# Six of a feed-forward block's last eight output tiles computed by Strassen's scheme, and two small pieces of work moved ahead of them

## The chip, the cores and the metric

The kernel runs on one core of a Trainium2 chip. The metric is the device time of one execution in microseconds (us), of which there are three for the kernel before. The program runs five engines side by side, which meet only at semaphores: TensorE (PE in the rows; PEld is its weight load), VectorE (DVE), ScalarE (ACT), GpSimd (POOL) and SyncE (SP), whose queue issues nearly all DMAs.

## The reference

Two transformer blocks run in sequence on 512 tokens of width 1024. The part in question is the feed-forward part of the first, and one norm of the second:

```
def _sq_relu_mlp(h, w1, w2):                       # w1: 1024 x 4096, w2: 4096 x 1024
    return jnp.square(jax.nn.relu(h @ w1)) @ w2
...
    y_x = _sq_relu_mlp(_modulate(x, g_pre_mlp[l], sh2, sc2), w_mlp_in[l], w_mlp_out[l])
    x = x + gt2 * _rmsnorm(y_x, g_post_mlp[l])
...
def mem_group(q_raw, mem_h, w_mem_kv, q_norm, k_norm):     # 256 memory rows, 4 heads of 128
    ...
    k = rmsnorm(kv[:, :, 0], k_norm)
...
    lb_all = jnp.cumsum(jax.nn.softmax(hg_lb_logits.astype(jnp.float32), axis=0), axis=0)
```

The first product gives 4096 inner features, the second sums over them to 1024 outputs. The memory keys are normed over 128 features per head. The "lower bounds" are a softmax over two rows of 512 numbers.

## The kernel before

**Numbers.** Activations lie transposed: 128 features on the partitions, tokens along the row. A product keeps float32 accuracy with three TensorE matmuls in the type fp32r: each operand is split into a high part (ACT copies it to fp32r) and a low part (the rest, subtracted by POOL or DVE), and `products` (L879, L880, L881) issues high x high, low x high and high x low into one PSUM bank. A plain output tile of 128 features is summed over its input tiles k in matmuls of 512 columns, one for each token.

**Strassen pairs.** Most tiles of the MLP are computed in pairs of output tiles by a scheme of seven products in place of eight: two output tiles by two halves of the tokens, over even and odd input tiles. A pair issues 7 products of 4 input pairs of 3 matmuls of 256 columns, that is 84. For each pair the other engines prepare seven weight pieces: `weight_sums` (DVE, L3087 to L3097) forms four sums of weight tiles; `piece_high` (ACT, L1824) copies the seven pieces q = 0 to 6 to fp32r; `piece_rest` (POOL, L3814) subtracts for q = 0, 1, 3, 5, 6 and `piece_low` (DVE, L2750) for q = 2, 4. Afterwards `first_product` (ACT), `product_sums` and `first_sum` (DVE, L3110 to L3122) join the seven products to two output tiles. ACT's copy of piece q for the next pair overwrites the buffer of piece q of the running pair, so it waits for that product:

```
            else:
                act.wait_ge(s.prod, 7 * (n - 1) + q + 1)
```

**The loop.** `FIRST_MLP` lists the pairs n = 0 to G-1. It goes in quarters of the 4096 inner features: "inner" pairs (two tiles of 128 features each, k from 2c to 2c+1, called c) and then "outer" pairs, which add a quarter's eight input tiles into all eight output tiles of `y`. Before, outer pairs 0 to 11 belong to quarters 0 to 2, four each; `OUTER[d]` is the place of outer pair d in the list, `INNER[p]` of inner pair p. An outer pair that comes first in its quarter (`first_out`: d = 0, 4, 8) issues three quarters of each product, and then the last quarters. ACT, DVE and POOL each run one loop over n with their work written out in order by hand; within iteration n they prepare pair n+1's pieces.

For an inner result of quarters 0 to 2, ACT squares (`even_squared`, `odd_squared`) and splits it, DVE adds four sums of 256 columns for the scheme's inputs (`form_sums`, L3197 to L3203), ACT copies them high (`sums_of_form_high`) and POOL subtracts twice (`form_sums_rest`, ySL). For quarter 3 (c = 12 to 15) it is split whole into `bH` and `bL` and no sums are formed.

**The last quarter's output.** Its eight tiles m = 0 to 7 are plain: m = 0 and 1 together, then 2 to 5, each 8 k of 3 matmuls of 512 columns; then m = 6 and 7 for the first 256 tokens and for the others, so that the norm of the first half can start. `ahead` splits chunks of 8 weight tiles (ACT L1815, POOL L3809). DVE adds each bank to `y` (L3288, L3306), ACT squares it, POOL sums the squares (`add_squares`, L3819, and `late_squares`). `half_statistic` (L1355, L1356) puts the sum over features on PE in the fifth step of tile 6's second half; then ACT takes the root, and `second_norm` (DVE L3320, L3323, L3328, ACT L1826) makes the next block's input from `y` and `xT`.

**What lies between those tiles.** After tiles 1 to 4, PE issues `statistic_of_halves("mk0".."mk3", 256)` (L951, L952): ones times the high and low parts of a head's squared keys. ACT squares and splits, DVE takes the rest (`low_sums`), ACT the root, DVE scales the key (L3294). The lower bounds take nine instructions on [128, 4] or [128, 8] (DVE L3270 to L3283, ACT L2279, L2280) ahead of tile 0's addition.

**SP's queue.** `weights_load(i)` loads 512 KB into one of four buffers `raw` once it is free. The residual `xT` (2 MB) is reloaded from DRAM ahead of load `last_inner`, after outer pair 11. It shares its memory with `yS`, the forms of an outer quarter.

Of the kernel before, what the change touches and what calls it, by code (L numbers as in the profile page):

```python
# [53 lines left out]
OUT_ORDER = [24 + i for i in (0, 1, 2, 3, 4, 5, 7, 6)]  # L54


def plan_weights():
# [73 lines left out]
    for c in range(0, len(plan), CB):  # L131
# [15 lines left out]
             + [("outer", 4 * quarter + j) for j in range(4 if quarter < 3 else 0)]]  # L147
# [210 lines left out]
def after_run(n):  # L358

    return len(SPLIT) if run_of(n) else number("w_mlp_out", OUT_ORDER[0], 0)  # L360
# [168 lines left out]
def _banks():  # L529
# [54 lines left out]
def build(nc, xt, xn, ctxt, memt, pos, wall, vec, cst, invc, hmask, rpbw, poolw, out):  # L584
# [275 lines left out]
    def tensor_program():  # L860
# [85 lines left out]
        def statistic_of_halves(name, n=512):  # L946
            o = claim(7)
# [381 lines left out]
        def XB(k):  # L1329
            return bH[:, k % 8, :], bL[:, k % 8, :], s.lo, LO.b + (k if k % 2 else k + 2)  # L1330

        outs = [claim(BANK["w_mlp_out", m]) for m in range(2)]
        for i, k in enumerate(OUT_ORDER):
            x_h, x_l, sem, value = XB(k)
            pe.wait_ge(sem, value)
            for m in range(2):
                w_h, w_l, raise_ = weights("w_mlp_out", k, m)
                mm = products(outs[m], w_h, w_l, x_h, x_l, i == 0, i == 7)
                if raise_:
                    mm.then_inc(s.product, 1)  # L1340
# [453 lines left out]
    def scalar_program():  # L1794
# [375 lines left out]
        def odd_high(c):  # L2170
# [5 lines left out]
            if c < 12:  # L2176
                copy(yH[:, c % 4, 256:768], squares_of(c)[1], s.hi)
            else:
                copy(bH[:, 2 * (c - 12) + 1, :], squares_of(c)[1], s.hi)

        def even_high(c):
            if c:
                act.wait_ge(s.relu_sq, 2 * c)
            if c < 12:
                copy(yH[:, c % 4, 0:256], squares_of(c)[0][:, 0:256], s.hi)
            else:
                copy(bH[:, 2 * (c - 12), :], squares_of(c)[0], s.hi)
# [2162 lines left out]
```

## Time and profile before

| | us |
|---|---|
| three runs | 1290.13, 1290.35, 1290.64 |
| median | 1290.35 |
| the profiled execution's own time | 1291.04 |
| its span | 1289.7 |
| PE busy in the span | 1278.8 |
| DVE, ACT, POOL busy | 964.3, 782.5, 807.2 |

The profile is of one execution. Its span runs from the first to the last instruction; its own time holds 1.34 us more. Times in its rows are from the span's start. A matmul's duration counts its way through the array, so the cost of one in a row of them is the distance from its start to the next start. "[0.81 <-PE bank L881]" behind a row says how long the engine was idle before it, and what ended that.

### The profile page before, as it was taken

The page shows a single profiled execution, that of the slowest core. Times are in us where ns is not written, and L with a number is a line of the kernel's source. Part 1 is how long each engine was busy: PE and PEld are TensorE (multiplying, and loading weights), DVE is VectorE, ACT ScalarE, POOL GpSimd, SP SyncE. Part 2 cuts the span into 40 slices and gives each one's busy share as a digit, 9 for nine tenths or more (in the row PEclk, how much of TensorE's full clock was granted, in tenths as well). Part 3 has the DMA queues.
Part 4 walks back from the last instruction along what each step waited for, and adds up shares of the span by engine and source line. Part 5 has one row for each costly group of instructions (what it writes and reads, how often), then busy time and mean ns, then how long its engine had stood idle before and what let it go on. Part 6 is the DMA issues. An engine that isn't in the chain of part 4 may idle for free.

```text
span 1289.7 us, 22877 instructions
## 1 busy us (share of the span) xinstructions
PE 1278.8 (99%) x8718; PEld 1136.6 (88%) x8718; DVE 964.3 (75%) x1692; ACT 782.5 (61%) x1488; POOL 807.2 (63%) x585
## 2 busy tenths in 40 slices
PE   9999999999999999999999999999999999999998
PEld 6788778879999999988788788777789999999998
DVE  5796695878778989834468575747589887987888
ACT  4532585479677585865655557645577655765664
POOL 3643333579778687656467373644378876877785
DMA  9685235353333323533332112120223333333333
GB/s 378 240 323 203 88 127 209 126 176 107 115 107 99 110 102 100 180 99 101 128 108 81 45 63 67 65 66 33 66 82 115 99 99 105 107 101 116 99 106 108
DMA packets 42125, 156.35 MB, mean 121 GB/s; under 512 B 4384, under 2 KB 5152, under 8 KB 40992
## 3 DMA queue, kind: packets, MB, share of 16 engines
q1 hardware_dynamic: 41136, 151.60, 34.2%
q0 software_dynamic: 448, 2.62, 0.5%
q8 instruction: 69, 1.13, 0.3%
q10 hardware_dynamic: 432, 0.67, 0.1%
q14 instruction: 40, 0.33, 0.1%
HBM read 149.90 MB, written 4.19 MB: 119 GB/s over the span
## 4 chain that ended last, share of the span: by engine, by line
PE 82%; DVE 10%; ACT 4%; POOL 2%; issue 2%; DMA 1%; DVEq 0%; SPq 0%; POOLq 0%; ACTq 0%
PE bank L879 23%; PE bank L881 22%; PE bank L880 22%; PE bank L1437 2%; PE bank L928 1%; PE bank L929 1%; PE bank L930 1%; PE bank L982 1%; DVE small L2940 1%; POOL wL L3814 1%; PE bank L942 1%; PE bank L975 1%; DVE P L2948 1%; PE bank L967 1%; PE bank L1674 1%
## 5 line engine op out<-in xcount | busy, mean ns | idle before, releaser
L3809 POOL TENSOR_TENSOR wL<-raw,wH 128x1024 fp32r<-128x1024 f32 (+1 forms) x91 | 223.3, 2459 | 239.9 <-ACT wH L1815 236.8
L879 PE MATMUL bank<-hH,wH 128*128 128x512 f32 (+1 forms) x544 | 211.0, 388 | 1.6 <-POOL wL L3809 0.6
L881 PE MATMUL bank<-hH,wL 128*128 128x512 f32 (+1 forms) x544 | 200.6, 369 | 0.0
L880 PE MATMUL bank<-hL,wH 128*128 128x512 f32 (+1 forms) x544 | 200.3, 368 | 0.0
L3814 POOL TENSOR_TENSOR wL<-raw,wH 128x512 fp32r<-128x512 f32 (+1 forms) x120 | 154.3, 1286 | 31.2 <-ACT wH L1824 30.5
L879 PE MATMUL bank<-gH,wH 128*128 128x256 f32 x512 | 145.4, 284 | 0.3 <-POOL gL L3814 0.3
L881 PE MATMUL bank<-gH,wL 128*128 128x256 f32 x512 | 144.9, 283 | 0.0
L880 PE MATMUL bank<-gL,wH 128*128 128x256 f32 x512 | 144.9, 283 | 0.0
L1815 ACT ACTIVATE wH<-raw 128x1024 fp32r<-128x1024 f32 (+1 forms) x91 | 95.1, 1047 | 53.7 <-PE bank L881 27.5
L879 PEld LDWEIGHTS bank<-hH,wH 128*128 128x128 f32 x544 | 102.9, 189 | 24.9 <-issue 6.5
L881 PEld LDWEIGHTS bank<-hH,wL 128*128 128x128 f32 x544 | 102.6, 189 | 18.0
L880 PEld LDWEIGHTS bank<-hL,wH 128*128 128x128 f32 x544 | 103.0, 189 | 15.3 <-issue 1.9
L3814 POOL TENSOR_TENSOR wL<-t,wH 128x512 fp32r<-128x512 f32 (+1 forms) x66 | 83.4, 1264 | 26.3 <-ACT wH L1824 25.9
L879 PEld LDWEIGHTS bank<-gH,wH 128*128 128x128 f32 x512 | 98.3, 192 | 0.7 <-POOL gL L3814 0.5
L2750 DVE TENSOR_TENSOR wL<-bank,wH 128x512 fp32r<-128x512 f32 (+1 forms) x118 | 79.7, 675 | 25.6 <-ACT wH L1824 25.6
L880 PEld LDWEIGHTS bank<-gL,wH 128*128 128x128 f32 x512 | 98.3, 192 | 0.2 <-issue 0.2
L881 PEld LDWEIGHTS bank<-gH,wL 128*128 128x128 f32 x512 | 98.3, 192 | 0.0
L3814 POOL TENSOR_TENSOR pL<-raw,pH 128x512 fp32r<-128x512 f32 (+1 forms) x60 | 77.4, 1289 | 27.8 <-ACT pH L1824 27.3
L1824 ACT ACTIVATE wH<-bank 128x512 fp32r<-128x512 f32 (+1 forms) x118 | 69.2, 586 | 42.1 <-DVE bank L3093 27.2
L1824 ACT ACTIVATE wH<-raw 128x512 fp32r<-128x512 f32 (+1 forms) x120 | 74.5, 621 | 33.2 <-PE bank L881 32.1
L3814 POOL TENSOR_TENSOR wL<-tmp,wH 128x512 fp32r<-128x512 f32 x52 | 67.8, 1304 | 25.4 <-ACT wH L1824 24.4
L879 PE MATMUL bank<-yH,wH 128*128 128x256 f32 x288 | 81.5, 283 | 0.0
(538 smaller groups left out, 4072.4 us busy)
## 6 DMA issues: line engine op xcount, KB each, us to landing
raw<-in_wall SPq DMA_DIRECT2D x211, 512.0 KB, 3.3
rows<-in_wall SPq DMA_DIRECT2D x24, 1024.0 KB, 11.3
bra<-in_rpbw SPq DMA_DIRECT2D x8, 360.0 KB, 4.5
xq<-in_xt SPq DMA_DIRECT2D x2, 1024.0 KB, 6.6
xT<-in_xn SPq DMA_DIRECT2D x1, 2048.0 KB, 7.9
out_x<-xT SPq DMA_DIRECT2D x1, 2048.0 KB, 8.8
xT<-out_x SPq DMA_DIRECT2D x1, 2048.0 KB, 9.2
out_x<-xT SPq DMA_DIRECT2D x6, 256.0 KB, 2.4
```

Source lines behind the costliest of these rows:

```text
L879: matmul(o, a_h, b_h, start=first, stop=False)
L880: matmul(o, a_h, b_l, start=False, stop=False)
L881: return matmul(o, a_l, b_h, start=False, stop=last)
L928: matmul(o, x_h, w_h, start=n == 0, stop=False)
L929: matmul(o, x_h, w_l, start=False, stop=False)
L930: mm = matmul(o, x_l, w_h, start=False, stop=n == len(ks) - 1)
L1437: mm = matmul(o[:, 64 * c:64 * c + 64], e_[:, 128 * c:128 * c + 128], view(e_[:, :], 128 * c + m, [[2 * m, 64 // m], [1, m]]), start=True, ...
L1815: activation(wH[i % NHL][:, 0:n], raw[r % NRAW][:, 0:n], ACT.Copy).then_inc(s.w_hi, 1)
L1824: activation(dst, src, ACT.Copy).then_inc(sem, 1)
L2750: tt(low, src, high.bitcast(F32), ALU.subtract).then_inc(sem, 1)
L3809: tt(wL[i % NHL][:, 0:n], raw[load(c) % NRAW][:, 0:n], wH[i % NHL][:, 0:n].bitcast(F32), ALU.subtract).then_inc(s.w_lo, 1)
L3814: tt(low, src, high.bitcast(F32), ALU.subtract).then_inc(sem, 1)
```

## The change

- **Outer pairs 12, 13 and 14** (output tiles 0 to 5 of the last quarter) join the loop; pair 12 is a `first_out` one, and the last of the loop is outer pair 14 and no longer inner pair 13. Tiles 6 and 7 stay plain and in halves. Inner results c = 12 to 15 get the sums of forms as all others. Since m = 6, 7 want the plain late tokens of the even tiles, these go to `xlast`, and ACT (`late_high`) and POOL split them (`xlH`, `xlL`, 128 x 1024) in iteration `OUTER[13]`.
- **Squares of y** follow as `result_square` (ACT) and `result_sum` (POOL) in the order `Y_ORDER`, with buffers `ysum` and `ysq` of their own.
- **The memory keys' norm** moves into quarter 0. ACT squares and splits all four heads at once at the end of iteration `OUTER[0]` (`memory_squares`, two instructions of 128 x 1024). POOL subtracts at the end of iteration `OUTER[1]`. PE issues the statistic in two parts of 512 columns, `mk0` after product q = 0 of `OUTER[2]` and `mk1` after product q = 0 of `OUTER[3]`. ACT takes the roots after `first_product` there and DVE scales (`memory_key`) before `product_sums`.
- **The lower bounds** become a generator of five steps, run after `OUTER[1]`, `[4]`, `[6]`, `[8]`, `[11]` on DVE, with ACT's two exponentials at the end of `OUTER[3]`.
- **SP:** the reload of `xT` goes as two DMAs of 1 MB, ahead of load `first_f + 2`, after `s.prod >= 7 * G`. The two loads of `hmask` wait for `xlL` in place of `mk3`. POOL's DMA of the positions waits for `mk1`.

```diff
@@ plan_weights
-        if quarter < 3:
-            for j in range(4):
-                for i, odd in ((0, 0), (1, 0), (1, 1), (0, 1)):
-                    tile("w_mlp_out", 2 * j + i, range(8 * quarter + odd, 8 * quarter + 8, 2))
-        else:
-            group([("w_mlp_out", m) for m in range(2)], OUT_ORDER)
-            for m in range(2, 8):
-                tile("w_mlp_out", m, OUT_ORDER)
+        for j in range(4 if quarter < 3 else 3):
+            for i, odd in ((0, 0), (1, 0), (1, 1), (0, 1)):
+                tile("w_mlp_out", 2 * j + i, range(8 * quarter + odd, 8 * quarter + 8, 2))
+    for m in (6, 7):
+        tile("w_mlp_out", m, OUT_ORDER)
@@ tensor_program
+        KEY_PLACE = {(OUTER[2], 0): 0, (OUTER[3], 0): 1}
+
+        def memory_statistic(i):
+            statistic_of_halves(f"mk{i}", 512, BANK["mk", i])
+            freed[BANK["mk", i]] = s.mk_n, 2 * i + 2
...
                     product_of(n, q, range(4), True, True).then_inc(s.prod, 1)
+                if (n, q) in KEY_PLACE:
+                    memory_statistic(KEY_PLACE[n, q])
...
-        for m in range(6):
-            b = BANK["w_mlp_out", m]
-            if m >= 2:
-                tile("w_mlp_out", m, OUT_ORDER, [(claim(b), XB)])
-            freed[b] = s.y_full, m + 1
-            if 0 < m < 5:
-                statistic_of_halves(f"mk{m - 1}", 256)
@@ scalar_program
+        def late_high():
+
+            act.wait_ge(s.relu_sq, 2 * 15)
+            act.wait_ge(s.prod, 7 * (INNER[13] + 1))
+            copy(xlH[:, :, :], xlast[:, :, :], s.full)
+
+        def memory_squares():
+            act.wait_ge(s.k_mem, 4)
+            activation(ksq[:, :], kvM[:, 0:2, :].rearrange("p a t -> p (a t)"), ACT.Square).then_inc(s.head_sq, 4)
+            act.wait_ge(s.head_sq, 4)
+            activation(ksqH[:, :], ksq[:, :], ACT.Copy).then_inc(s.sums_hi, 2)
+
+        def memory_root(i):
+            root_of(f"mk{i}", 128, bank[BANK["mk", i]], bank[BANK["mk", i]])
+
+        def result_square(i):
+
+            act.wait_ge(s.y, Y.half + 24 + i + 1)
+            if i > 2:
+                act.wait_ge(s.add_g, ADD_G.f + i - 2)
+            square((ysq[i % 2] if i else ysum)[:, :], y[:, Y_ORDER[i], :], s.sq)
...
             first_product(n)
+            if outer_of(n) in (2, 3):
+                memory_root(outer_of(n) - 2)
             piece_high(n + 1, 2)
...
+            if outer_of(n) == 13:
+                late_high()
             piece_high(n + 1, 3)
...
             piece_high(n + 1, 6)
+            if outer_of(n) == 13:
+                result_square(0)
+                result_square(1)
...
             if n + 2 < G:
                 even_columns(n + 2)
+            if outer_of(n) == 0:
+                memory_squares()
@@ vector_program
+        def memory_key(i):
+            dve.wait_ge(s.root, rooted(f"mk{i}"))
+            dve.wait_ge(s.ones, 5)
+            stt(out=kvM[:, i, :], in0=kvM[:, i, :], scalar=vc("mem_k"), in1=bank[BANK["mk", i]],
+                op0=ALU.mult, op1=ALU.mult).then_inc(s.mk_n, 2)
...
                 piece_low(n + 1, 2)
+            if outer_of(n) in (2, 3):
+                memory_key(outer_of(n) - 2)
             product_sums(n)
@@ gpsimd_program
+        def result_sum(i):
+            pool.wait_ge(s.sq, SQ.f + i + 1)
+            if i > 1:
+                pool.wait_ge(s.add_g, ADD_G.f + i - 1)
+            tt(ysum[:, :], ysum[:, :], ysq[i % 2][:, :], ALU.add).then_inc(s.add_g, 1)
...
             piece_rest(n + 1, 3)
+            if outer_of(n) == 13:
+                pool.wait_ge(s.full, FULL.b + 33)
+                rest(xlL[:, :, :], xlast[:, :, :], xlH[:, :, :], s.rest_g)
...
             piece_rest(n + 1, 5)
             piece_rest(n + 1, 6)
...
+            if outer_of(n) == 1:
+                pool.wait_ge(s.sums_hi, halved("mk1") + 1)
+                tt(ksqL[:, :], ksq[:, :], ksqH[:, :].bitcast(F32), ALU.subtract).then_inc(s.sums_lo, 2)
@@ sync_program
-            if i == last_inner:
-                sp.wait_ge(s.prod, outer_done(2))
+            if i == first_f + 2:
+                sp.wait_ge(s.prod, 7 * G)
                 sp.wait_ge(s.x_moved, 32)
-                nc.sync.dma_start(xT[:, :, :], out).then_inc(s.x_moved, 16)
+                nc.sync.dma_start(xT[:, 0:4, :], out[:, 0:4, :]).then_inc(s.x_moved, 16)
+                nc.sync.dma_start(xT[:, 4:8, :], out[:, 4:8, :]).then_inc(s.x_rest_in, 16)
```

## Rows read from the trace of the kernel before

**Rows 1.** The page: head, busy time, and the chain that ended last.

```profile
span 1289.7 us, 22877 instructions
PE 1278.8 (99%) x8718; PEld 1136.6 (88%) x8718; DVE 964.3 (75%) x1692; ACT 782.5 (61%) x1488; POOL 807.2 (63%) x585
PE 82%; DVE 10%; ACT 4%; POOL 2%; issue 2%; DMA 1%; DVEq 0%; SPq 0%; POOLq 0%; ACTq 0%
```

**Rows 2.** Busy time by stretches: an inner pair of quarter 2; the six tiles.

```profile
core 0: us, PE busy (x) PEld busy (x) DVE busy (x) ACT busy (x) POOL busy (x), PEclk, DMA share, GB/s
558.59:592.29 33.70, 33.70 (x154) 27.98 (x153) 10.15 (x24) 17.91 (x34) 20.33 (x11) 1.00 0.31 104
447.50:457.60 10.10, 10.10 (x86) 10.10 (x86) 8.63 (x18) 8.90 (x18) 7.30 (x7) 1.00 0.34 105
```

**Rows 3.** PE's timeline around tiles 0 to 5 (start, duration, engine).

```profile
558.47 0.28 PE L881 MATMUL bank<-hH,wL 128*128 128x256 f32 x1
558.59 0.40 PE L879 MATMUL bank<-bH,wH 128*128 128x512 f32 x1
...
569.49 0.28 PE L951 MATMUL bank<-sumH,ones 128*128 128x256 f32 x1
569.61 0.28 PE L952 MATMUL bank<-sumL,ones 128*128 128x256 f32 x1
569.73 0.40 PE L879 MATMUL bank<-bH,wH 128*128 128x512 f32 x1
...
592.29 0.28 PE L879 MATMUL bank<-bH,wH 128*128 128x256 f32 x1
592.41 0.28 PE L880 MATMUL bank<-bL,wH 128*128 128x256 f32 x1
```

**Rows 4.** PE's timeline where outer pairs 1, 9 and 2 start.

```profile
325.88 0.28 PE L881 MATMUL bank<-yH,wL 128*128 128x256 f32 x1
326.10 0.39 PE L879 MATMUL bank<-yH,pH 128*128 128x256 f32 x1
326.32 0.28 PE L880 MATMUL bank<-yA,pH 128*128 128x256 f32 x1
...
487.53 0.28 PE L881 MATMUL bank<-yH,wL 128*128 128x256 f32 x1
487.93 0.39 PE L879 MATMUL bank<-yH,pH 128*128 128x256 f32 x1
...
336.27 0.28 PE L879 MATMUL bank<-yH,pH 128*128 128x256 f32 x1
337.71 0.28 PE L879 MATMUL bank<-yH,wH 128*128 128x256 f32 x1
```

**Rows 5.** ACT's timeline in iteration `OUTER[1]`, and a chunk's copy.

```profile
330.31 0.61 ACT L1824 ACTIVATE pH<-raw 128x512 fp32r<-128x512 f32 x1
336.47 0.63 ACT L1824 ACTIVATE wH<-tmp 128x512 fp32r<-128x512 f32 x1 [0.81 <-PE bank L881]
...
553.31 1.05 ACT L1815 ACTIVATE wH<-raw 128x1024 fp32r<-128x1024 f32 x1
```

**Rows 6.** POOL's timeline in iteration `OUTER[1]`, and a chunk's rest.

```profile
331.01 1.31 POOL L3814 TENSOR_TENSOR pL<-raw,pH 128x512 fp32r<-128x512 f32 x1
332.26 1.33 POOL L3814 TENSOR_TENSOR wL<-raw,wH 128x512 fp32r<-128x512 f32 x1
337.18 1.30 POOL L3814 TENSOR_TENSOR wL<-tmp,wH 128x512 fp32r<-128x512 f32 x1
...
554.43 2.40 POOL L3809 TENSOR_TENSOR wL<-raw,wH 128x1024 fp32r<-128x1024 f32 x1 [3.73 <-ACT wH L1815]
```

**Rows 7.** The whole span's waits of PE's weight load: us in total, times, longest.

```profile
PEld bank L1046 <- DVE xsq L2806: 2.0, 2, 1.5
```

**Rows 8.** The norm behind tiles 6 and 7: PE, DVE and POOL.

```profile
599.85 0.59 PE L1355 MATMUL bank<-acc,ones 128*128 128x256 f32 x2
...
602.47 0.43 DVE L3323 TENSOR_TENSOR bank<-xT,bank 128x256 f32<-128x256 f32 x1
...
593.99 1.29 POOL L3819 TENSOR_TENSOR acc<-acc,tmp 128x512 f32<-128x512 f32 x1 [1.61 <-ACT tmp L1839]
```

**Rows 9.** The page's DMA issues: KB each, median us from issue to landing.

```profile
rows<-in_wall SPq DMA_DIRECT2D x24, 1024.0 KB, 11.3
xq<-in_xt SPq DMA_DIRECT2D x2, 1024.0 KB, 6.6
xT<-out_x SPq DMA_DIRECT2D x1, 2048.0 KB, 9.2
```

More of the change, by code:

```diff
@@ L50 @@
 GROUPS = ((0, 8), (8, 16), (16, 22))
-OUT_ORDER = [24 + i for i in (0, 1, 2, 3, 4, 5, 7, 6)]
+OUT_ORDER = range(24, 32)
+Y_ORDER = (1, 0, 3, 2, 5, 4)
 def plan_weights():
@@ L146 @@
              for pair in [("inner", p) for p in range(max(0, 4 * quarter - 2), 4 * quarter + 2)]
-             + [("outer", 4 * quarter + j) for j in range(4 if quarter < 3 else 0)]]
+             + [("outer", 4 * quarter + j) for j in range(4 if quarter < 3 else 3)]]
 INNER = {i: at for at, (kind, i) in enumerate(FIRST_MLP) if kind == "inner"}
@@ L358, in after_run @@
 def after_run(n):
[L360 removed]
+    return len(SPLIT) if run_of(n) else number("w_mlp_out", OUT_ORDER[0], 6)
 def reach(name, k, m, chunks=NHL):
@@ L441 @@
 MULT = before(hc=8, h2=8, b=3)
-FULL = before(first=16, hm=8, h2=4, b=24, fs=22)
+FULL = before(first=16, hm=8, h2=4, b=33, fs=22)
 REST = before(first=8, hm=4, h2=8, fs=22)
-REST_G = before(first=8, hm=4, s2=4, b=24, form=4, fb=22)
+REST_G = before(first=8, hm=4, s2=4, b=33, form=4, fb=22)
 X2_S = before(x2=8, up=22)
@@ L458, in normed @@
     return NORMS.index((which, j - j % 2))
-ROOTS = ("x ctx mem mix pre_mlp mk0 mk1 mk2 mk3 post_a post_b h3 mq hg0 hg1 hg2 hg3 lq lk q k "
+ROOTS = ("x ctx mem mix pre_mlp mk0 mk1 post_a post_b h3 mq hg0 hg1 hg2 hg3 lq lk q k "
          "om ol ffn").split()
@@ L469, in rooted @@
     return 2 * ROOTS.index(name) + 2
-HALVED = "mk0 mk1 mk2 mk3 lq".split()
+HALVED = "mk0 mk1 lq".split()
 def halved(name):
@@ L552, in _banks @@
         of.update((("sum", p, j), of["sum", p - (2 - j // 2), (1, 3, 0, 2)[j]]) for j in range(4))
-    held = [of["sum", G - 2, 1], of["sum", G - 2, 3], of["sum", G - 1, 2]]
-    of.update((("w_mlp_out", m), b) for m, b in enumerate(held + held + [2, 3]))
+    of.update({("w_mlp_out", 6): 2, ("w_mlp_out", 7): 3})
+    of.update({("mk", i): of["sum", OUTER[2 + i] - 1, 1] for i in range(2)})
     of.update({("vt", 0): 4, ("vt", 1): 6})
@@ L678, in build @@
     xl = at("xl", R + 92 * K, [128, 256])
+    xlast = at("xl", 88 * K, [128, 4, 256])
+    xlH = at("xlH", R + 56 * K, [128, 4, 256], F32R)
+    xlL = at("xlL", R + 60 * K, [128, 4, 256], F32R)
+    ysum = at("ysum", R + 72 * K, [128, 512])
+    ysq = [at("ysq", R + (74 + 2 * i) * K, [128, 512]) for i in range(2)]
     sS = [at("sS", R + (24 + 4 * i) * K, [128, 1024]) for i in range(2)]
@@ L1327, in tensor_program, with XB @@
             first_freed(n)
[L1329 to L1340, printed above, removed]
-        for m in range(6):
-            b = BANK["w_mlp_out", m]
-            if m >= 2:
-                tile("w_mlp_out", m, OUT_ORDER, [(claim(b), XB)])
-            freed[b] = s.y_full, m + 1
-            if 0 < m < 5:
-                statistic_of_halves(f"mk{m - 1}", 256)
+        def XB(k, i):
+            c = 12 + (k - 24) // 2
+            if k % 2:
+                return yH[:, c % 4, 256 + 256 * i:512 + 256 * i], yB[c % 4][:, i, :], s.lo, LO.b + 2 * c + 1
+            if i:
+                return xlH[:, c % 4, :], xlL[:, c % 4, :], s.rest_g, REST_G.b + 33
+            return yH[:, c % 4, 0:256], yA[c % 4][:, :], s.lo, LO.b + 2 * c + 2
         freed[2] = freed[3] = s.piece_v, 2 * G
@@ L2175, in odd_high @@
             forms_free(c)
[L2176 to L2179, printed above, removed]
+            copy(yH[:, c % 4, 256:768], squares_of(c)[1], s.hi)
         def even_high(c):
@@ L2183, in even_high @@
                 act.wait_ge(s.relu_sq, 2 * c)
[L2184 to L2187, printed above, removed]
+            copy(yH[:, c % 4, 0:256], squares_of(c)[0][:, 0:256], s.hi)
         def sums_of_form_high(c, side):
@@ L3184, in form_sums @@
             x_, y_ = squares_of(c)
-            late = xl[:, :] if c else tm[1][:, 256:512]
+            late = tm[1][:, 256:512] if c == 0 else xl[:, :] if c < 12 else xlast[:, c - 12, :]
             s1, s4, s3, s2 = (yS[c % 4][:, 256 * n:256 * n + 256] for n in range(4))
@@ L3947, in gpsimd_program @@
             if n + 1 == G:
-                ahead("w_mlp_out", 24, 0, 2)
+                result_sum(1)
+                ahead("w_mlp_out", OUT_ORDER[0], 6, 2)
+                result_sum(2)
+                result_sum(3)
                 continue
@@ L3958, in gpsimd_program @@
             piece_rest(n + 1, 6)
-        for m in range(8):
-            if m not in (1, 7):
-                ahead("w_mlp_out", OUT_ORDER[4 if m == 0 else 0], m)
-            if 0 < m < 6:
-                if m > 1:
-                    pool.wait_ge(s.add_g, ADD_G.f + m - 1)
-                add_squares(acc[0][:, :], m, s.sq, SQ.f)
+            if outer_of(n) == 1:
+                pool.wait_ge(s.sums_hi, halved("mk1") + 1)
+                tt(ksqL[:, :], ksq[:, :], ksqH[:, :].bitcast(F32), ALU.subtract).then_inc(s.sums_lo, 2)
+        result_sum(4)
+        result_sum(5)
         def late_squares(i):
```

191 lines of the change are left out of this document (79 added, 112 removed).

## The prediction, on record before the changed kernel was run

> **What bounds the kernel.** I read the page's head first: TensorE is busy for 1278.8 of 1289.7 us, and the chain that ended last is PE for 82% [rows 1]. Then the stretches: in an inner pair of quarter 2 and in the six tiles PE is busy for the whole stretch at the granted clock 1.00, that is 2.4 GHz, while POOL has 2.8 to 13 us left [rows 2]. So a us of matmuls taken away is a us of span, and a wait that PE did not have is lost whole: no later wait of PE is long enough to take it up, the longest of its weight load being 1.5 us in the whole span, and none of any size lies in the first MLP [rows 7, 4]. The question is then how many us of matmuls go, and whether PE meets a new wait.
>
> **The matmuls removed and added.** The six tiles are 6 x 8 x 3 = 144 matmuls of 512 columns and the four statistics 8 of 256. They stand from 558.59 to 592.29: 33.70 us. The first 48 take 569.49 - 558.59 = 10.90, so 0.227 us each; one of 256 columns takes 0.120 (569.49 to 569.61) [rows 3]. 144 x 0.227 + 8 x 0.12 = 33.65, which closes. In their place come 3 pairs x 84 x 0.120 = 30.24, and 4 statistic matmuls of 512 columns in quarter 0, 4 x 0.227 = 0.91. That is -33.70 + 30.24 + 0.91 = -2.55 us. So Strassen's eighth is only 2.5 us here: a matmul half as wide costs more than half.
>
> The rule for back-to-back matmuls in the Trainium skill ("TensorE: Matmul & The Clock Gate", section on the back-to-back issue gap) is columns / 2.4 + 2.5 ns, 216 ns for 512 columns and 109 for 256. The trace disagrees by 11 ns at both widths. An estimate by that page would be 144 x 0.216 + 8 x 0.109 = 31.98 before and 252 x 0.109 + 4 x 0.216 = 28.33 after, -3.6 in place of -2.55, and the total below would be 1291.2. I take the trace.
>
> **A small wait behind a first outer pair.** Where a pair follows a `first_out` one, POOL has two ySL subtractions ahead of the new pair's piece 0, and PE starts late: outer pair 1 by 326.32 - 325.88 - 0.24 = 0.20 us, outer pair 9 by 0.40 + 0.22 - 0.24 = 0.38 with the same slow second start [rows 4]. Outer pair 13 is now such a pair. Bounds 0.20 and 0.38; quarter 3 is like quarter 2, so near the upper, +0.3.
>
> **The statistic in `OUTER[2]`: a new wait.** PE issues mk0 behind product 0 of outer pair 2, and it needs ksqL, which POOL makes at the end of iteration `OUTER[1]`, behind piece 6 of pair 2. ACT's copy of piece 6 waits for the last product of outer pair 1. The trace shows this wait end at 336.47, just behind the end of that pair; POOL's subtraction starts at 337.18 and takes its turn of 1.26 [rows 5, 6]. PE, though, starts pair 2 at 336.27 and is done issuing product 0 at 337.71 [rows 4]. The work that PE needs can't even begin by then.
>
> When does it end? I move the engines' rows by what is inserted.
> ACT: `memory_squares` starts where the copy of piece 0 now stands, 330.31. Each of its two instructions is 128 x 1024 from SBUF, for which the nearest row is 1.05 [rows 5]; with the wait of the second for the first, the copy of piece 0 starts at 332.4 and ends at 333.0.
> POOL: piece 0 at 333.1 (now 331.01), then pieces 1, 3, 5, 6 back to back at turns of 1.25 (331.01 to 332.26) [rows 6]: piece 6 at 338.1, ksqL at 339.35. ACT has made up its delay by piece 6, for which it waits anyway. ksqL is a subtraction of 128 x 1024 as at 554.43, 2.40 [rows 6]: it ends at 341.75.
> PE goes on at 341.75 and pays 0.1 for a weight load that couldn't run ahead, as at 326.10 to 326.32 [rows 4]. PE's loss is 341.85 - 337.7 = 4.15 us.
> Bounds: if `memory_squares` cost POOL nothing, ksqL would run from 338.45 to 340.85, 3.2 us of wait. If POOL's and ACT's new instructions took half as long again in company, it is 4.15 + 1.2 + 1.0 = 6.4. I take the worked value. Behind PE only TensorE's own products wait; the other engines use the time to get ahead, so nothing else grows. Nothing brings it back either.
>
> **What I cost at nothing, and its cover.**
> mk1 in `OUTER[3]`: its low part comes with mk0's. It claims the bank of pair 2's sum, which ACT copies to `y` some 0.2 us before PE comes: between 0 and 0.3.
> ACT's two roots and DVE's two scalings: each 0.6 to 0.9 us, in outer pairs of quarter 0 where ACT waits for PE 0.8 us at a time [rows 5]; DVE's `product_sums` moves by 0.8, but its result is wanted by ACT only 1.4 later. Without that cover a bank comes late by 0.8.
> The lower bounds: nine instructions of 0.15 to 0.2 us, one to three per outer pair. Tile 0's addition is gone, behind which they were hidden before, so nothing is saved.
> Forms of quarter 3: DVE +4 sums of 256 columns, POOL +2 subtractions, ACT +2 copies per inner pair. That is what quarter 2 does already, where DVE is busy for 8.63, ACT for 8.90 and POOL for 7.30 of 10.10 and PE does not wait [rows 2].
> Iteration `OUTER[13]`: ACT +1.05 (`late_high`) and two squares, POOL +2.40 (xlL) between pieces 3 and 5. Piece 6 is then ready some 3 us into pair 14 and wanted after 8.6. The chunk of tile 6 is ready on POOL 1.7 us before PE reaches it.
> The norm's chain: PE comes to `half_statistic(0)` at 599.85, 7.56 behind the start of tile 6 at 592.29 [rows 8, 3]. Now four more sums of 1.29 [rows 8] stand on POOL behind the chunk of tile 7, and end 5.8 behind that start; the last two squares need 0.7 more, so 6.8 with ACT: 0.8 to spare. If the spare is gone, each us over it is a us of span.
> SP: the reload of xT starts when tile 6 does and is wanted 602.47 - 592.29 = 10.2 later [rows 8, 3]. 1 MB landed in 6.6 (xq), 2 MB in 9.2 (xT), 1 MB in a crowd in 11.3 (rows) [rows 9]: hidden, or 1.1 late at worst. The weight loads `first_f + 2`, `+ 3` and the hmask loads now queue behind it, and land by some 14 us after tile 6's start; ACT takes them at 15 and 17.
>
> **The sum.** -2.55 + 0.30 + 4.15 = +1.9 us. The profiled execution (span 1289.7, own time 1291.04) would become 1291.6 and 1292.9. Its own time is 0.69 above the median of the runs; the difference carries over: 1290.35 + 1.9 = **1292.25 us**.
>
> About 0.2%, 2.6 us, is what a measurement of this kernel can tell from no change. The forecast lies inside.
>
> **The rivals.**
> A, on the other side (slower): the clock. PE has never stood for 4 us in this trace; through all waits up to 1.5 the granted clock stayed 1.00 [rows 7, 2]. If this wait lets it fall to 1.2 GHz, the products behind it take double: 12 x 0.12 = 1.44 more for one product at that clock, 2.9 for two. Total +3.3 to +4.8: 1293.7 to 1295.1. It decides from 0.7 us on, six matmuls at half clock. For: the length of the wait. Against: before and behind it PE is busy without a break.
> The Trainium skill ("TensorE: Matmul & The Clock Gate", Part 1 on the clock gate) states that the clock halves after an idle stretch and is given back after sustained work. No run here shows it yet; by that rule rival A is what happens, if 4 us is idle enough.
> B (slower): one of the covers fails: DVE in quarter 3, which starts behind three bound steps, the norm's chain, or xT. Each is worth 1 to 2 us: about 1293.8. For: the spare of the norm's chain and of xT is worked out, not seen. Against: every one has a row of a like stretch that keeps time.
> C: the wait isn't there, because ksqL is done in time. Then -2.25: 1288.1, still within 0.2%. For: nothing but that POOL's spans are rough. Against: ACT's wait at 336.47 [rows 5] holds it whatever POOL's speed.
> D (faster by over 0.2%): no wait, and the norm's chain gains as well, since tile 6's neighbours leave ACT and POOL more room: 1287 or less.
>
> **How the numbers follow.** Forecast 0.56, A 0.19, B 0.12, C 0.08, D 0.05. A tenth of the forecast's own cases (a wait above 4.8) lies over +2.6. Slower by over 0.2%: 0.19 + 0.12 + 0.05 = 0.36. Faster: 0.05. Within: 0.59. The range leaves out C and D (0.13) below and the far end of A above: from 1290.3 (the wait at its lower bound of 3.2, the step behind pair 12 at 0.2, less 0.9 for what else is off) to 1295.2 (A with two products). The forecast's own range is 1291.3 to 1294.5, from the two bounds of the wait.
>
> **What would show it.** In the new profile: three more pairs of 10.1 us on PE; tile 6 starting 30.5 us behind the end of inner pair 13; in quarter 0 PE idle once for about 4 us, behind product 0 of the outer pair 2 near 338 us, ended by POOL's subtraction of 128 x 1024; two matmuls of 512 columns behind it; the second statistic without a wait; the granted clock in the 10 us behind it (1.00 for the forecast, less for A); the distance from tile 6's start to L1355 still 7.6 us. The prediction is wrong if the wait isn't there or is half as long, or if pairs of quarter 3 take more than 10.1 us.

## The result, and the profile after

The changed kernel takes 1297.78 us (median of six runs, 1296.92 to 1298.53), the kernel before 1290.30 (six runs, 1290.12 to 1291.00): ratio 1.0055, 95% interval 1.0044 to 1.0066. That is 7.5 us slower. I had forecast 1292.25, with a range to 1295.2.

The page's head, the counterpart of [rows 1]:

```profile
span 1296.0 us, 23202 instructions
PE 1281.1 (99%) x8822; PEld 1143.2 (88%) x8822; DVE 989.5 (76%) x1735; ACT 791.7 (61%) x1512; POOL 825.8 (64%) x604
PE 74%; DVE 14%; ACT 5%; issue 3%; POOL 3%; DMA 1%; DVEq 0%; SPq 0%; ACTq 0%; POOLq 0%
```

PE's share of the chain that ended last fell from 82% to 74%, and DVE's rose from 10% to 14%. That is a hint that more than one long wait happened: the chain leaves PE more often.

To find where, I follow PE's starts, as in [rows 3, 4], at the forecast wait (start, duration, engine):

```profile
336.78 0.28 PE L889 MATMUL bank<-yH,pL 128*128 128x256 f32 x1
341.02 0.77 PE L959 MATMUL bank<-ksqH,ones 128*128 128x512 f32 x1 [3.96 <-POOL ksqL L3974]
341.58 0.63 PE L960 MATMUL bank<-ksqL,ones 128*128 128x512 f32 x1
342.01 0.42 PE L887 MATMUL bank<-yH,wH 128*128 128x256 f32 x1
...
346.91 0.28 PE L889 MATMUL bank<-yH,wL 128*128 128x256 f32 x1
...
598.63 0.28 PE L887 MATMUL bank<-yH,wH 128*128 128x256 f32 x1
...
606.19 0.67 PE L1360 MATMUL bank<-ysum,ones 128*128 128x256 f32 x2
```

The wait is 341.02 - 336.78 - 0.12 = 4.12 us, ended by `ksqL`, the POOL subtraction named in the prediction. But behind it the distance from start to start is 0.21 in place of 0.12. Windows over the same stretch show why:

```profile
336.90:341.00 4.10, 0.16 (x2) 0.01 (x1) 4.07 (x5) 1.43 (x3) 4.10 (x4) 0.89 0.39 128
341.00:347.00 6.00, 5.98 (x26) 5.82 (x27) 3.07 (x5) 1.23 (x2) 2.39 (x2) 0.51 0.28 90
347.00:357.00 10.00, 10.00 (x84) 9.91 (x83) 6.56 (x12) 7.05 (x13) 5.19 (x4) 1.00 0.17 52
```

The column behind POOL's is the granted clock: 0.51 from 341 to 347, which is the 1.2 GHz level, and 1.00 again from 347. The two matmuls of 512 columns take 342.01 - 341.02 = 0.99 in place of 2 x 0.227, and the 23 behind them 346.91 - 342.01 = 4.90 in place of 23 x 0.12 = 2.76. Together that is 0.54 + 2.14 = 2.68 us. Of these, 0.11 is not the clock's: behind a wait at the full clock the same two matmuls take 0.57 and not 0.454 (342.39 - 341.82 in the second experiment), which is the 0.1 that the prediction counted for a weight load that can't run ahead. The clock's own part is 2.57. The Trainium skill ("TensorE: Matmul & The Clock Gate", Part 1) says that the clock halves after an idle stretch and returns after sustained work; the trace agrees, with 0.51 behind 4.12 us of standing still and 1.00 behind the 5.9 us of work that followed.

POOL's timeline, the counterpart of [rows 6], has the order that I worked out, all of it some 0.8 us earlier, as PE's pairs are here in this execution:

```profile
332.29 1.29 POOL L3814 TENSOR_TENSOR pL<-raw,pH 128x512 fp32r<-128x512 f32 x1 [2.00 <-ACT pH L1830]
...
337.31 1.27 POOL L3814 TENSOR_TENSOR wL<-tmp,wH 128x512 fp32r<-128x512 f32 x1
338.53 2.34 POOL L3974 TENSOR_TENSOR ksqL<-ksq,ksqH 128x1024 fp32r<-128x1024 f32 x1
```

DVE's timeline has rows that I had no term for. The first two are steps of the lower bounds behind `OUTER[1]`, the next three those behind `OUTER[4]` and `OUTER[6]`; the row at 446.41 is three steps of the positions' angles, which stood behind `OUTER[7]` before as well, and the last is where `product_sums` of inner pair 7 starts:

```profile
337.41 1.19 DVE L3239 TENSOR_TENSOR lb<-vecs,lb 128x4 f32<-128x4 f32 x1
338.52 2.37 DVE L3240 TENSOR_TENSOR lb<-vecs,lb 128x4 f32<-128x4 f32 x1
...
417.94 0.92 DVE L3243 TENSOR_TENSOR lb<-lb 128x4 f32<-128x4 f32 x1
418.90 0.18 DVE L3245 RECIPROCAL lb<-lb 128x4 f32<-128x4 f32 x1
...
438.09 0.76 DVE L3248 TENSOR_TENSOR lb<-lb 128x4 f32<-128x4 f32 x1
...
446.41 4.69 DVE L3151 SCALAR_TENSOR_TENSOR tmp<-tmp 128x512 f32<-128x512 f32 x3
...
465.78 0.41 DVE L3113 TENSOR_TENSOR acc<-bank,rs 128x256 f32<-128x256 f32 x1
```

A subtraction of 4 elements per partition takes 2.37 us, and it ends at 340.89, when POOL's `ksqL` ends (338.53 + 2.34 = 340.87); the one ahead of it ends at 338.60, and POOL's piece at 338.58. The same instructions in the kernel before took 0.155 and 0.161, at 562 us, where POOL had nothing to do. The kernel before, POOL's timeline there:

```profile
564.63 4.75 POOL L3809 TENSOR_TENSOR wL<-raw,wH 128x1024 fp32r<-128x1024 f32 x2 [5.11 <-ACT wH L1815]
```

and operations on `lb`, by line:

```profile
L3272 DVE TENSOR_TENSOR lb<-vecs,lb x1: 161/161/161, 562.3 to 562.3; 128x4 f32<-128x4 f32 x1
L3273 DVE TENSOR_TENSOR lb<-vecs,lb x1: 155/155/155, 562.4 to 562.4; 128x4 f32<-128x4 f32 x1
L3275 DVE TENSOR_TENSOR lb<-lb x1: 163/163/163, 562.9 to 562.9; 128x4 f32<-128x4 f32 x1
...
L3281 DVE TENSOR_SCALAR lb<-lb x1: 169/169/169, 563.5 to 563.5; 128x4 f32<-128x4 f32 x1
```

(The three numbers are the shortest, median and longest duration in ns, then follow the first and last start.) Finally PE's new short waits in quarters 2 and 3, the rows that have a releaser:

```profile
464.99 0.38 PE L887 MATMUL bank<-hH,pH 128*128 128x256 f32 x1 [0.49 <-DVE yB L2753]
...
495.81 0.39 PE L887 MATMUL bank<-yH,wH 128*128 128x256 f32 x1 [0.28 <-POOL ySL L3814]
497.05 0.39 PE L887 MATMUL bank<-yH,pH 128*128 128x256 f32 x1 [0.27 <-POOL pL L3814]
...
578.37 0.39 PE L887 MATMUL bank<-yH,pH 128*128 128x256 f32 x1 [0.26 <-POOL pL L3814]
```

Each costs what its start lies too late, and 0.10 more, since the next start is 0.22 behind it, as in [rows 4]. In quarter 2 the seven of them (464.99: 0.74; 475.16 and 485.32: 0.08 each; 493.18: 0.34; 494.55: 0.31; 495.81: 0.54; 497.05: 0.53) make 2.62, of which 0.38 was there before [rows 4, outer pair 9]: 2.24. In quarter 3 two (577.13: 0.16; 578.37: 0.52) make 0.68.

So from the last matmul of outer pair 0 (325.07) to the first of tile 6 (598.63) 273.56 us pass, where it was 592.29 - 325.88 = 266.41 [rows 3, 4]. The 7.15 us are -2.55 + 4.12 + 2.68 + 2.24 + 0.68 = 7.17. Behind tile 6 nothing moved: from there to the end of the span are 697.37 us, before 697.41. The difference of the spans is 6.3 and not 7.15 because outer pair 0 ended 0.8 earlier in the execution profiled after. That execution's own time, 1297.33, is 0.45 below its median, and the one before was 0.69 above: 6.3 + 0.45 + 0.69 is the 7.4 to 7.5 between the medians.

### The profile page after: what moved, and what is told of

Read it like the earlier page. It is cut to its first block, busy times and chain, and to the rows that moved or that the text cites. A ratio compares the mean times of both kernels' runs of the same rounds, so it can differ in the third digit from the quotient of the medians.

```text
span 1296.0 us, 23202 instructions
## 1 busy us (share of the span) xinstructions
PE 1281.1 (99%) x8822; PEld 1143.2 (88%) x8822; DVE 989.5 (76%) x1735; ACT 791.7 (61%) x1512; POOL 825.8 (64%) x604
## 3 DMA queue, kind: packets, MB, share of 16 engines
q0 software_dynamic: 448, 2.62, 0.5%
## 4 chain that ended last, share of the span: by engine, by line
PE 74%; DVE 14%; ACT 5%; issue 3%; POOL 3%; DMA 1%; DVEq 0%; SPq 0%; ACTq 0%; POOLq 0%
PE bank L887 20%; PE bank L889 19%; PE bank L888 19%; PE bank L1443 2%; PE bank L936 1%; PE bank L938 1%; PE bank L937 1%; PE bank L990 1%; DVE bank L3118 1%; DVE small L2943 1%; PE bank L950 1%; DVE bank L3096 1%; PE bank L983 1%; POOL wL L3814 1%; PE bank L975 1%
## 5 line engine op out<-in xcount | busy, mean ns | idle before, releaser
L3809 POOL TENSOR_TENSOR wL<-raw,wH 128x1024 fp32r<-128x1024 f32 (+1 forms) x85 | 208.7, 2460 | 223.0 <-ACT wH L1821 219.9
L3814 POOL TENSOR_TENSOR wL<-raw,wH 128x512 fp32r<-128x512 f32 (+1 forms) x126 | 162.3, 1289 | 32.2 <-ACT wH L1830 31.7
L1821 ACT ACTIVATE wH<-raw 128x1024 fp32r<-128x1024 f32 (+1 forms) x85 | 89.0, 1048 | 53.7 <-PE bank L889 27.5
L887 PE MATMUL bank<-yH,wH 128*128 128x256 f32 x384 | 110.2, 287 | 0.3 <-POOL ySL L3814 0.3
L889 PE MATMUL bank<-yH,wL 128*128 128x256 f32 x384 | 109.6, 285 | 0.0
L2753 DVE TENSOR_TENSOR wL<-bank,wH 128x512 fp32r<-128x512 f32 (+1 forms) x124 | 83.7, 675 | 33.2 <-ACT wH L1830 33.2
L1830 ACT ACTIVATE wH<-bank 128x512 fp32r<-128x512 f32 (+1 forms) x124 | 72.7, 587 | 47.8 <-DVE bank L3096 34.2
L3814 POOL TENSOR_TENSOR pL<-raw,pH 128x512 fp32r<-128x512 f32 (+1 forms) x63 | 81.2, 1289 | 28.8 <-ACT pH L1830 28.2
L1830 ACT ACTIVATE wH<-raw 128x512 fp32r<-128x512 f32 (+1 forms) x126 | 78.3, 621 | 32.5 <-PE bank L889 31.3
```

The costliest lines, as they stand in the source:

```text
L887: matmul(o, a_h, b_h, start=first, stop=False)
L889: return matmul(o, a_l, b_h, start=False, stop=last)
L1821: activation(wH[i % NHL][:, 0:n], raw[r % NRAW][:, 0:n], ACT.Copy).then_inc(s.w_hi, 1)
L1830: activation(dst, src, ACT.Copy).then_inc(sem, 1)
L2753: tt(low, src, high.bitcast(F32), ALU.subtract).then_inc(sem, 1)
L3809: tt(wL[i % NHL][:, 0:n], raw[load(c) % NRAW][:, 0:n], wH[i % NHL][:, 0:n].bitcast(F32), ALU.subtract).then_inc(s.w_lo, 1)
```

## The experiments

Theories ahead of them: the long wait costs its 4.1 and a fallen clock 2.7 (W with the clock); the lower bounds, stretched by POOL, make DVE late in quarter 2 (L); against L, that quarter 2's waits are a late effect of the stop at 341, which shifted the engines against each other (K). In the expectations below, C is the rival that the clock falls for another reason than the wait.

### The keys' low part ahead of pair 2's pieces

```diff
@@ gpsimd_program, iteration OUTER[1]
+            if outer_of(n) == 1:
+                pool.wait_ge(s.sums_hi, halved("mk1") + 1)
+                tt(ksqL[:, :], ksq[:, :], ksqH[:, :].bitcast(F32), ALU.subtract).then_inc(s.sums_lo, 2)
             piece_rest(n + 1, 0)
             piece_rest(n + 1, 1)
...
             piece_rest(n + 1, 6)
-            if outer_of(n) == 1:
-                pool.wait_ge(s.sums_hi, halved("mk1") + 1)
-                tt(ksqL[:, :], ksq[:, :], ksqH[:, :].bitcast(F32), ALU.subtract).then_inc(s.sums_lo, 2)
```

> The changed kernel with one instruction moved on GpSimd: the low part of the squared keys is taken ahead of the first piece of outer pair 2 and not behind its last. Theory W (PE's one wait in outer pair 2, and the fall of the clock behind it, cost 4.1 + 2.7 us; the short waits of quarters 2 and 3, some 2.8 us, have another cause): no idle time of PE above 0.5 us in outer pair 2, granted clock 1.00 there, 1297.8 - 6.9 = 1290.9 us. Rival K (the later short waits are knock-on effects of that wait): they go too, 1289 us or less, or 1288.5. Rival C (the clock falls for another reason than the wait): 1293.6.

Measured: 1291.81 us (1291.03 to 1292.13) beside 1290.40 for the kernel before, ratio 1.0009 (1.0000 to 1.0017). From the changed kernel's time that is -6.0. POOL's timeline:

```profile
332.44 2.41 POOL L3962 TENSOR_TENSOR ksqL<-ksq,ksqH 128x1024 fp32r<-128x1024 f32 x1 [1.57 <-ACT ksqH L2208]
334.81 1.30 POOL L3814 TENSOR_TENSOR pL<-raw,pH 128x512 fp32r<-128x512 f32 x1
```

and PE's:

```profile
337.84 0.50 PE L959 MATMUL bank<-ksqH,ones 128*128 128x512 f32 x1
...
459.55 0.38 PE L887 MATMUL bank<-hH,pH 128*128 128x256 f32 x1 [0.42 <-DVE yB L2753]
```

The wait and the half clock (4.12 + 2.68 = 6.80) are gone, and the granted clock is 1.00 over the whole execution; a late piece 0 takes 0.27 of it back, and the two statistics 0.20 and 0.41, by the distances of PE's starts. 6.80 - 0.88 = 5.9. K falls: without any stop in quarter 0, the wait on `yB` in inner pair 8 is still there (0.42), and `product_sums` of inner pair 7 starts 11.45 us into its pair, as after the change (11.51: 465.78 less the pair's start of 454.27), where the kernel before had 9.33.

### Sixteen matmuls in the wait

```diff
@@ tensor_program, memory_statistic
+            if i == 0:
+                o = claim(BANK["mk", 0])
+                pe.wait_ge(s.sums_hi, halved("mk1") + 1)
+                for _ in range(16):
+                    matmul(o, ones_r[:, :], HALVES["mk0"][1], start=True, stop=True)
```

> The changed kernel with its wait left in place, but PE kept busy through it: ahead of the wait for the low part it issues 16 matmuls of 512 columns (3.6 us) into the bank that the statistic overwrites. The output is unchanged. Theory W: PE goes on at the same time as in the changed kernel, some 4 us late, but at the full clock; only the clock's part comes back, -2.7: 1295.1 us. Rival C (the clock falls for another reason, or the products behind the wait are slow for want of operands): about 1297.8.

Measured: 1294.61 us (1294.52 to 1295.58), ratio 1.0034 (1.0021 to 1.0047); -3.2 from the changed kernel. PE's timeline, and the window behind it:

```profile
337.59 0.28 PE L889 MATMUL bank<-yH,pL 128*128 128x256 f32 x1
338.06 3.92 PE L1326 MATMUL bank<-ksqH,ones 128*128 128x512 f32 x16 [0.19 <-ACT y L1835]
341.82 0.50 PE L959 MATMUL bank<-ksqH,ones 128*128 128x512 f32 x1
342.16 0.40 PE L960 MATMUL bank<-ksqL,ones 128*128 128x512 f32 x1
342.39 0.28 PE L887 MATMUL bank<-yH,wH 128*128 128x256 f32 x1
```

```profile
342.00:348.00 6.00, 6.00 (x49) 5.91 (x50) 3.42 (x6) 3.75 (x7) 2.32 (x2) 1.00 0.26 90
```

The statistic comes 341.82 - 337.59 = 4.23 us behind product 0, to be read beside 4.24 after the change: the wait is whole, but PE has work in it, and the clock stays at 1.00. From product 0's last matmul to tile 6 the trace is 2.66 us shorter than the changed kernel's (596.78 - 337.59 = 259.19 beside 598.63 - 336.78 = 261.85): the 2.57 worked out from the rows, and nearly 0.1 of shorter waits in quarter 2. So 2.6 us are the clock's, and they can be had back without touching the wait. The medians differ by 0.5 more than the rows explain; the five runs lie 1.1 us apart.

### The lower bounds in quarter 0

```diff
@@ vector_program
-            if outer_of(n) in (1, 4, 6, 8, 11):
-                next(bound)
+            for _ in range({1: 1, 3: 4}.get(outer_of(n), 0)):
+                next(bound)
@@ scalar_program
-            if outer_of(n) == 3:
+            if outer_of(n) == 2:
```

> The changed kernel, wait included, with the five steps of the lower bounds put into quarter 0 alone (one behind outer pair 1, four behind outer pair 3; ACT's exponentials behind outer pair 2). Theory L (small VectorE instructions with both operands in SBUF wait for GpSimd's running instruction, 0.5 to 1.2 us each, and in quarters 1 and 2 VectorE has no time left): product_sums at the start of quarter 2 comes 9.3 us and not 11.4 into a pair, the waits of PE between 460 and 498 us shrink from 2.3 to 0.4 us: 1297.8 - 1.9 = 1295.9 us. Rival K (those waits follow from the long wait in outer pair 2): 1297.8.

Measured: 1295.11 us (1293.98 to 1295.67), ratio 1.0035 (1.0022 to 1.0049); -2.7 from the changed kernel. `product_sums` of inner pair 7 starts 9.32 into its pair again (463.95 - 454.63), and of quarter 2's waits one is left, that which the kernel before had. DVE's timeline, and PE's:

```profile
463.95 0.41 DVE L3113 TENSOR_TENSOR acc<-bank,rs 128x256 f32<-128x256 f32 x1
```

```profile
494.83 0.28 PE L889 MATMUL bank<-yH,wL 128*128 128x256 f32 x1
495.25 0.39 PE L887 MATMUL bank<-yH,pH 128*128 128x256 f32 x1
```

From product 0's last matmul to tile 6 it is 2.21 us less than after the change (259.64), as the 2.24 of quarter 2 would have it. The instructions were not made shorter but put where DVE has time: there the multiplication (L3248) took 1.20 us, and nobody waited for it.

### Both

The first experiment's edit and the third's together.

> Both edits together: the keys' low part early on GpSimd, and the lower bounds in quarter 0. Theories W and L: only the waits behind the first outer pairs are left, so -2.55 for the columns and +0.7 for quarter 3 against the kernel of before: about 1288.8 us (1288.3 to 1289.5). If a cost of the change has been missed: 1290 or more.

Measured: 1288.99 us (1288.57 to 1289.54) beside 1290.40, ratio 0.9990 (0.9981 to 0.9998). This is faster than both kernels, than the one before by an interval that just leaves out 1. Its rest is explained by its rows: -2.55 for the columns; a late piece 0 in outer pair 2 (336.26) 0.26, the two statistics 0.20 and 0.04; the step in quarter 3 0.72. That sums to -1.33, measured -1.4.

The 0.04 at the second statistic shows something that the first experiment hid, where it was 0.41. There the second subtraction of the lower bounds behind `OUTER[1]` took 1.33 us beside POOL's piece, and here, in the same place, 0.15: it starts at 339.80, and POOL's piece at 339.82. In the first experiment they start at 339.82 and 339.84. What decides between 0.15 and 1.33 is less than these rows resolve. With the 1.33, DVE is 1.2 us later at the end of outer pair 2, and ACT's copy that frees the bank of the second statistic is late: this bound step costs PE 0.37 where PE does not stand in `OUTER[2]`.

### The keys' low part in the middle of the pieces

```diff
@@ gpsimd_program, iteration OUTER[1]
                 form_sums_rest(c, 1)
+            if outer_of(n) == 1:
+                pool.wait_ge(s.sums_hi, halved("mk1") + 1)
+                tt(ksqL[:, :], ksq[:, :], ksqH[:, :].bitcast(F32), ALU.subtract).then_inc(s.sums_lo, 2)
             piece_rest(n + 1, 5)
             piece_rest(n + 1, 6)
-            if outer_of(n) == 1:
-                pool.wait_ge(s.sums_hi, halved("mk1") + 1)
-                tt(ksqL[:, :], ksq[:, :], ksqH[:, :].bitcast(F32), ALU.subtract).then_inc(s.sums_lo, 2)
```

> The changed kernel with the keys' low part on GpSimd ahead of piece 5 of outer pair 2, two pieces earlier than in the changed kernel. PE should wait about 1.6 us in outer pair 2 in place of 4.1. Theory W: the clock falls only behind the long wait, so it stays at 1.00: 1297.8 - 2.5 - 2.7 = 1292.6 us, or, from the kernel with the early low part (1291.8), 1291.8 + 1.4 = 1293.2. Rival: a wait of 1.6 us is enough for the clock to fall: 1295.3 to 1295.9.

Measured: 1292.76 us (1291.99 to 1293.44), ratio 1.0014 (1.0005 to 1.0023). PE's wait, and the windows around it:

```profile
338.49 0.47 PE L959 MATMUL bank<-ksqH,ones 128*128 128x512 f32 x1 [1.52 <-POOL ksqL L3972]
```

```profile
336.00:342.00 6.00, 4.48 (x36) 4.22 (x35) 5.96 (x8) 2.46 (x6) 6.00 (x5) 1.00 0.22 63
342.00:348.00 6.00, 6.00 (x52) 6.00 (x51) 5.37 (x11) 4.32 (x10) 3.56 (x4) 1.00 0.36 120
```

PE stands for 338.49 - 336.69 - 0.12 = 1.68 us, and the clock stays at 1.00.

### Eight matmuls in the wait

The edit of the second experiment, with `range(8)`.

> As the run that filled the long wait with 16 matmuls, but with 8 (1.8 us), so that some 2.0 us of the wait stay idle behind them. The output is unchanged. If an idle stretch of 2 us leaves the clock alone, the time is that of the run with 16: 1294.6 us, granted clock 1.00. If it takes the clock down, it is that of the changed kernel: 1297.3 to 1297.8.

Measured: 1294.68 us (1294.44 to 1295.28), ratio 1.0031 (1.0019 to 1.0043). PE's timeline, and the window behind it:

```profile
337.24 2.11 PE L1326 MATMUL bank<-ksqH,ones 128*128 128x512 f32 x8 [0.18 <-ACT y L1835]
340.96 0.50 PE L959 MATMUL bank<-ksqH,ones 128*128 128x512 f32 x1 [1.61 <-POOL ksqL L3979]
```

```profile
342.00:348.00 6.00, 6.00 (x53) 6.00 (x52) 3.43 (x7) 3.88 (x8) 2.21 (x3) 1.00 0.24 90
```

Half the work does as much as all of it: PE stands for 340.96 - 337.24 - 8 x 0.227 = 1.90 us behind it, and the clock stays at 1.00. Of the stops tried here only the one of 4.12 us brought it down; where between the two it turns wasn't tried.

### The keys' low part between pieces 1 and 3, and the bounds in quarter 0

The edit of the fifth experiment with the three lines ahead of `piece_rest(n + 1, 3)`, and that of the third.

> The lower bounds in quarter 0 as in the run with both edits, and the keys' low part on GpSimd between pieces 1 and 3 of outer pair 2, where no piece is late for PE: the 0.3 us by which PE waited for piece 0 of pair 2 go, and some of the 0.25 at the second statistic: 1289.0 - 0.4 = 1288.6 us. If GpSimd's order costs PE elsewhere: 1289.0 or more.

Measured: 1289.50 us (1288.73 to 1289.88) beside 1290.79, ratio 0.9989 (0.9980 to 0.9998). I had hoped for 0.4 more than "both" gives; it is the same (-1.3 beside -1.4). Piece 0 is in time now, but the statistic waits in its place, in PE's timeline:

```profile
338.12 0.47 PE L959 MATMUL bank<-ksqH,ones 128*128 128x512 f32 x1 [0.29 <-POOL ksqL L3966]
```

### The early low part, and bounds with one operand

Beside the first experiment's edit:

```diff
@@ vector_program, lower_bounds
-            tt(lb[:, 0, :], lb[:, 1, :], lb[:, 2, :], ALU.add).then_inc(s.lb_v, 1)
+            nc.vector.reciprocal(lb[:, 0, :], lb[:, 1, :]).then_inc(s.lb_v, 1)
...
-            tt(lb[:, 3, :], lb[:, 1, :], lb[:, 0, :], ALU.mult).then_inc(s.lb_v, 1)
+            nc.vector.reciprocal(lb[:, 3, :], lb[:, 1, :]).then_inc(s.lb_v, 1)
...
-            ts(lb[:, 2, :], lb[:, 3, :], -1.0, 1.0, ALU.mult, ALU.add).then_inc(s.lb_v, 1)
+            nc.vector.reciprocal(lb[:, 2, :], lb[:, 3, :]).then_inc(s.lb_v, 1)
```

> The kernel with the keys' low part early (1291.8 us), and three of the small instructions of the lower bounds, behind outer pairs 4, 6 and 8, replaced in their places by a reciprocal with one operand of the same size (128 x 4), so the lower bounds are computed falsely and nothing else is left out. As many instructions, semaphores and waits as before. Theory L (an instruction with two operands in SBUF waits for GpSimd's running one): each falls to about 0.18 us, VectorE's product_sums at the start of quarter 2 comes 1.3 us earlier in its pair, and PE's waits there go for the most part: 1289.8 us. Rival (the steps cost VectorE their issue and semaphore waits): 1291.8.

Measured: 1290.01 us (1289.30 to 1290.66) beside 1290.79, ratio 0.9995 (0.9986 to 1.0003). The first experiment, from which it differs by these three lines alone, stood 1.4 above the kernel before; this one stands 0.8 below. The groups of the first experiment, and then of this one:

```profile
L3243 DVE TENSOR_TENSOR lb<-lb x1: 886/886/886, 412.6 to 412.6; 128x4 f32<-128x4 f32 x1
L3248 DVE TENSOR_TENSOR lb<-lb x1: 743/743/743, 432.7 to 432.7; 128x4 f32<-128x4 f32 x1
L3251 DVE TENSOR_SCALAR lb<-lb x1: 483/483/483, 494.8 to 494.8; 128x4 f32<-128x4 f32 x1
```

```profile
L3243 DVE RECIPROCAL lb<-lb x1: 171/171/171, 412.7 to 412.7; 128x4 f32<-128x4 f32 x1
L3248 DVE RECIPROCAL lb<-lb x1: 171/171/171, 432.1 to 432.1; 128x4 f32<-128x4 f32 x1
L3251 DVE RECIPROCAL lb<-lb x1: 171/171/171, 493.6 to 493.6; 128x4 f32<-128x4 f32 x1
```

The same places, the same size: 0.17 each. POOL runs a piece beside the first two here as well (412.30 to 413.61 and 431.54 to 432.84); the third starts within 0.05 us of the end of one. `product_sums` of inner pair 7 is back from 11.45 to 9.54, and the wait on `yB` is gone. So the number and the place of the instructions, with their semaphores, were not what cost; their kind was. For the first two the run changes two things at once, two operands to one and the operation to a reciprocal, and does not tell these apart. The Trainium skill ("SBUF — State Buffer", section "Who interferes with whom") says that a VectorE instruction with two SBUF inputs contends with a GpSimd one that reads SBUF, that the ports they share are an exclusive lock, and that the order of issue decides which of them blocks. The trace agrees on the two-operand ones, down to their ends at 340.89 beside POOL's 340.87. The one with a single operand and two constants (L3251) also ends with POOL's piece in the first experiment, at 495.32 beside 495.29, after 0.48 us; it took 0.17 with POOL idle, and 0.17 in its place of the third experiment, where POOL was at no subtraction. Why it waits isn't settled by these runs.

## Why the prediction was wrong

**Right: the matmuls.** Three pairs of 10.08 us; from the start of outer pair 12 (567.71) to tile 6 are 30.92 us, which are the 30.24 of the sum and 0.68 of waits. In "both", where the other costs are small, the sum closes with -2.55 to 0.1 us. By the issue gap that the prediction took from the Trainium skill, the estimate would have been 1 us too low; that section gives it for a single matmul, and another spacing for a stream with weight loads.

**Right: the wait in `OUTER[2]`.** Forecast 4.15 with the 0.1 for the weight load, measured 4.12 + 0.11 = 4.23, behind product 0 and ended by `ksqL`; the turns of ACT and POOL (1.25 a piece, 2.3 for `ksqL`) were as worked out. The first experiment shows that it is the place in POOL's order alone. mk1 cost 0.04, within its 0 to 0.3.

**Wrong: the clock behind it, costed at 0.** "The granted clock in the 10 us behind it (1.00 for the forecast, less for A)": it was 0.51 for 5.9 us. Rival A had the mechanism, with 0.19 for its chance, and 1.44 to 2.9 for its price; it cost 2.57 by the rows, and 2.66 of the second experiment's trace. My argument against it, that PE is busy without a break before and behind the wait, was no evidence: the trace of before held no stop longer than 1.5 us [rows 7], and the runs show that stops of that length (1.68 and 1.90) say nothing on one of 4.12. For an unseen wait of that length, the chance of A should have been the larger one.

**Wrong: "The lower bounds: nine instructions of 0.15 to 0.2 us, one to three per outer pair".** The range had room for the clock, with A in it, and none for this. With either cost taken away the kernel measured inside the range (1294.61 and 1295.11); both together took it out. The durations were read where POOL stood idle; moved into outer pairs, the two-operand ones run beside POOL's subtractions and took 0.3 to 2.4. The three in `OUTER[1]` cost nothing more, as PE stood anyway; where it did not stand, in the first experiment, they cost 0.37. Those behind `OUTER[4]` and `OUTER[6]` took 0.92 + 0.18 + 0.76 = 1.86, and the three steps of the angles at 446.41 then 4.69 in place of 4.20, together 2.35; `product_sums` came 2.2 later into its pair. In quarter 2 the loop of ACT and DVE needs 10.16 us a pair (the starts at 464.99, 475.16 and 485.32) beside PE's 10.08, so nothing of the delay was made up. PE's new waits there are 2.24. The third experiment shows the cause by its place, the last one by its kind; that nothing is made up at 10.16 is read from these rows and was not tested. The instructions were short and not on PE's path; what I didn't ask is how far DVE was from being on it. The row that I quoted, busy for 8.63 of 10.10, speaks of the engine's free time and not of the loop's.

**Undersized: the step behind pair 12.** 0.30 forecast, 0.68 measured: two late starts and not one. It stays in all versions (0.72 in "both").

**Right: the covers behind it.** Tile 6 to the norm's statistic is 606.19 - 598.63 = 7.56 us, as before; the reload of `xT` and SP's order cost nothing, since the rest of the span is the same to 0.04. Rivals C and D did not occur. B had looked for a DVE made late by bound steps, but in quarter 3, at 1 to 2 us; it was late in quarter 2, of which the prediction had said that PE does not wait.

With every term at its measured size the forecast would have been +1.9 + 0.08 + 2.57 + 2.24 + 0.38 = +7.2; the traces give +7.15, the medians +7.5.

## What to carry to other kernels

When a small piece of work is moved, read its duration off a row with the same neighbours: with two operands in SBUF it can last as long as what POOL is doing, and it is then as costly as the slack of the loop that it lands in, not as its engine's idle share. Ask of each new PE wait of several us what clock the work behind it gets, and price it at both levels; if the wait can't go, a few matmuls without use in it are cheaper than the clock. Work that was moved for the sake of a 2.5 us saving here brought 9.7 us of new costs, all of which but 1.2 could be had back by two changes of order.

## What the runs showed of the hardware that I had not expected

VectorE instructions on 128 x 4 elements took up to 2.37 us beside a GpSimd subtraction of 128 x 1024; two that took 0.89 and 0.74 beside subtractions of 128 x 512 took 0.17 in the same places as reciprocals of a single operand. TensorE's clock fell to 0.51 behind one stop of 4.12 us and was back at 1.00 behind 5.9 us of work, at a loss of 2.57 us; stops of 1.68 us, and of 1.90 us behind eight matmuls without use, left it at 1.00.
